# Head norms by logarithm and exponential, in one stage per layer, and plain splits by two engines, in a 32-bit transformer kernel

## What is computed

```
def rms_norm(x, gain):
    xf = x.astype(jnp.float32)
    y = xf * lax.rsqrt(jnp.mean(xf * xf, axis=-1, keepdims=True) + NORM_EPS)
    return (y * gain.astype(jnp.float32)).astype(x.dtype)

q = rms_norm(to_heads(h @ w_q, XM_HEADS), q_norm)
k = rms_norm(to_heads(k, XM_HEADS), k_norm)
...
x = x + from_heads(o) @ w_o
```

## Time and profile before

| | |
|---|---|
| Median of 3 runs | 5059.5 us (5055.14 to 5059.69) |
| Profiled execution, its own time | 5057.54 us |
| Its span | 5055.7 us |
| TensorE products, busy | 4678.1 us (93%) |
| VectorE, busy | 2261.2 us (45%) |
| ScalarE, busy | 1444.6 us (29%) |
| GpSimd, busy | 1938.2 us (38%) |
| Granted TensorE clock, mean | 0.963 |

### The profile page before, as it was taken

The page is one execution under the profiler, slowest core; times in us unless marked ns, Lnnn a source line. Parts: engine busy times, 40 slices in busy tenths (PEclk is TensorE's granted clock), DMA queues, the critical chain, the costliest instruction groups (busy, mean ns, idle before and its releaser), DMA issues. The chain is left out here.

```text
span 5055.7 us, 51526 instructions
## 1 busy us (share of the span) xinstructions
PE 4678.1 (93%) x19788; PEld 3543.7 (70%) x19788; DVE 2261.2 (45%) x4552; ACT 1444.6 (29%) x2163; POOL 1938.2 (38%) x884
## 2 busy tenths in 40 slices
PE   7667889999999999999999988899999997787999
PEld 6224757888888788888788745668878874355787
DVE  8697346983333233333440253454234136654440
ACT  3302322334444211111322234332222232233321
POOL 3054414446666444444444400334444431012443
PEclk9788989999999999999999989999999999998999
DMA  3011313445545656555222200212222221011222
GB/s 113 25 29 46 111 34 102 132 137 178 175 163 179 200 187 191 184 188 181 88 96 96 96 23 14 84 63 94 93 92 96 95 86 40 17 53 54 90 96 84
DMA packets 213172, 519.23 MB, mean 103 GB/s; under 512 B 16960, under 2 KB 82752, under 8 KB 210112
## 3 DMA queue, kind: packets, MB, share of 16 engines
q1 hardware_dynamic: 128448, 448.82, 27.0%
q10 hardware_dynamic: 84480, 67.12, 4.2%
HBM read 446.66 MB, written 69.21 MB: 102 GB/s over the span
## 5 line engine op out<-in xcount | busy, mean ns | idle before, releaser
L187 POOL TENSOR_TENSOR ring_rounded<-ring,highs_rounded 128x1024 fp32r<-128x1024 f32 x687 | 1683.7, 2452 | 2767.2 <-ACT highs_rounded L181 2767.2
L395 PE MATMUL bank<-arena_rounded,ring_rounded 128*128 128x512 f32 (+1 forms) x4488 | 1790.9, 399 | 99.6 <-DVE hT_rounded L413 41.4
L397 PE MATMUL bank<-arena_rounded,highs_rounded 128*128 128x512 f32 (+1 forms) x4488 | 1776.9, 396 | 0.0
L181 ACT ACTIVATE highs_rounded<-ring 128x1024 fp32r<-128x1024 f32 x687 | 727.9, 1061 | 2107.3 <-PE bank L397 1605.5
L396 PE MATMUL bank<-hT_rounded,highs_rounded 128*128 128x512 f32 x3128 | 1228.5, 393 | 0.0
L395 PEld LDWEIGHTS bank<-arena_rounded,ring_rounded 128*128 128x128 f32 x4488 | 854.0, 190 | 293.4 <-issue 86.1
L397 PEld LDWEIGHTS bank<-arena_rounded,highs_rounded 128*128 128x128 f32 x4488 | 852.6, 190 | 205.1
L396 PE MATMUL bank<-arena_rounded,highs_rounded 128*128 128x512 f32 (+1 forms) x2112 | 821.5, 389 | 0.0
L396 PEld LDWEIGHTS bank<-hT_rounded,highs_rounded 128*128 128x128 f32 x3128 | 593.3, 190 | 141.4
L396 PEld LDWEIGHTS bank<-arena_rounded,highs_rounded 128*128 128x128 f32 x2112 | 402.1, 190 | 86.9
L1248 DVE TENSOR_TENSOR arena<-qT,arena 128x512 f32<-128x512 f32 x64 | 150.6, 2354 | 372.2 <-ACT qT L1213 371.6
(11 more groups left out here) (325 smaller groups left out, 4684.9 us busy)
## 6 DMA issues: line engine op xcount, KB each, us to landing
ring<-pages_in SPq DMA_DIRECT2D x687, 512.0 KB, 3.4
act_table<-arena SPq DMA_DIRECT2D x128, 256.0 KB, 4.0
gate_table<-qT SPq DMA_DIRECT2D x16, 2048.0 KB, 7.3
arena<-act_table ACTq DMA_DIRECT2D x128, 256.0 KB, 4.0
arena<-gate_table ACTq DMA_DIRECT2D x32, 1024.0 KB, 8.4
arena<-ssm_in SPq DMA_DIRECT2D x16, 256.0 KB, 2.6
arena<-mem_in SPq DMA_DIRECT2D x3, 1024.0 KB, 4.8
xT<-x_in SPq DMA_DIRECT2D x8, 256.0 KB, 6.4
```

The source lines that it names most:

```text
L181: nc.scalar.activation(f32r(page_high(p)), slot(p), ACT.Copy).then_inc(masked_pages.sem, 1)
L187: nc.gpsimd.tensor_tensor(f32r(slot(p)), slot(p), part_of(page_high(p)), ALU.subtract).then_inc(split_pages.sem, 1)
L395: low_last = nc.tensor.matmul(out, f32r(w_low), f32r(x_high), start=start, stop=False)
L397: return low_last, nc.tensor.matmul(out, f32r(w_high), f32r(x_high), start=False, stop=stop)
```

## The change

It has three parts.

1. In `head_norm` the stage begins with a load of the set that holds both logarithm and exponential. After the last sum, ScalarE takes the logarithm of mean plus epsilon and then the exponential of minus half of it. VectorE makes mean plus epsilon while the exponential runs, and then does the Newton step. The reciprocal is gone.
2. `head_norm` takes units of different lengths. The queries and keys of the memory attention and of the two cross attentions are normed in one stage. There are 8 stages now.
3. In the plain split ScalarE makes the high parts, ahead of its page copies, and VectorE only subtracts.

```diff
-        def inverse_root(link, rms, psum, scale, eps, a, b):
-            link(nc.vector.tensor_scalar(a, psum, scale, eps, ALU.mult, ALU.add))
-            link(nc.vector.reciprocal(rms, rms))
-            link(nc.vector.tensor_tensor(b, rms, rms, ALU.mult))
-            link(nc.vector.scalar_tensor_tensor(out=b, in0=b, scalar=-0.5, in1=a, op0=ALU.mult, op1=ALU.mult))
-            link(nc.vector.scalar_tensor_tensor(out=rms, in0=b, scalar=1.5, in1=rms, op0=ALU.add, op1=ALU.mult))
...
@@ project, ScalarE @@
                         done += min(count, 3)
+                    elif split:
+                        for k in range(nk):
+                            nc.scalar.activation(f32r(high(k)), src(k), ACT.Copy).then_inc(masked_h.sem, 1)
                     for use, part, b, j, need in blocks():
...
@@ project, VectorE @@
                     elif split:
 
-                        for k in range(nk + 1):
-                            if k < nk:
-                                masked(high(k), src(k)).then_inc(masked_h.sem, 1)
-                            if k >= 1:
-                                dve.wait_ge(masked_h.sem, masked_h.at(k))
-                                nc.vector.tensor_tensor(f32r(src(k - 1)), src(k - 1), part_of(high(k - 1)),
-                                                        ALU.subtract).then_inc(h_split.sem, 1)
+                        for k in range(nk):
+                            dve.wait_ge(masked_h.sem, masked_h.at(k + 1))
+                            nc.vector.tensor_tensor(f32r(src(k)), src(k), part_of(high(k)),
+                                                    ALU.subtract).then_inc(h_split.sem, 1)
...
-        def head_norm(units, n, width, rope=None, at=(0, 3584), newton=newton):
+        def head_norm(units, width, rope=None, at=(0, 3584), newton=newton):
...
-            rms = small[0:32, 0:n]
+            rms = small[0:32, :]
+            mean = newton[0:32, 0, :]
             count = len(units)
+            long = [unit[0][0].shape[1] for unit in units]
...
                 def _(act):
+                    nc.scalar.preload_act_table_set("natural_log_exp_and_others")
                     for u, (chunks, window, gain) in enumerate(units):
...
-                            last = nc.scalar.activation(sq[:, u % 2, c, 0:n], ch, ACT.Square)
+                            last = nc.scalar.activation(sq[:, u % 2, c, 0:long[u]], ch, ACT.Square)
...
-                    nc.scalar.activation(rms, bank[0][0:32, 0:n], ACT.Sqrt, bias=gcol("eps")[0:32],
-                                         scale=1.0 / width).then_inc(rooted.sem, 1)
+                    nc.scalar.activation(rms, bank[0][0:32, :], ACT.Ln, bias=gcol("eps")[0:32],
+                                         scale=1.0 / width).then_inc(act_step.sem, 1)
+                    act.wait_ge(act_step.sem, act_step.at(1))
+                    nc.scalar.activation(rms, rms, ACT.Exp, scale=-0.5).then_inc(rooted.sem, 1)
...
+                    dve.wait_ge(act_step.sem, act_step.at(1))
+                    nc.vector.tensor_scalar(mean, bank[0][0:32, :], 1.0 / width, EPS, ALU.mult, ALU.add)
                     dve.wait_ge(rooted.sem, rooted.at(1))
-                    inverse_root(link, rms, bank[0][0:32, 0:n], 1.0 / width, EPS, newton[0:32, 0, 0:n],
-                                 newton[0:32, 1, 0:n])
+                    b = newton[0:32, 1, :]
+                    link(nc.vector.tensor_tensor(b, rms, rms, ALU.mult))
+                    link(nc.vector.scalar_tensor_tensor(out=b, in0=b, scalar=-0.5, in1=mean, op0=ALU.mult,
+                                                        op1=ALU.mult))
+                    link(nc.vector.scalar_tensor_tensor(out=rms, in0=b, scalar=1.5, in1=rms, op0=ALU.add,
+                                                        op1=ALU.mult))
                     dve.sem_inc(inverted.sem, 1)
...
-        head_norm([([Q(2 * h), Q(2 * h + 1)], ALL, "mem_q_g") for h in range(4)], SEQ, 256)
-        head_norm([([kT[:, 2 * h, 0:MEM], kT[:, 2 * h + 1, 0:MEM]], ALL, "mem_k_g")
-                   for h in range(4)], MEM, 256)
+        head_norm([([Q(2 * h), Q(2 * h + 1)], ALL, "mem_q_g") for h in range(4)]
+                  + [([kT[:, 2 * h, 0:MEM], kT[:, 2 * h + 1, 0:MEM]], ALL, "mem_k_g") for h in range(4)], 256)
...
-            head_norm([([Q(h)], ALL, f"xm_q_norm{layer}") for h in range(4)], SEQ, 128)
-            head_norm([([kT[:, h, 0:MEM]], ALL, f"xm_k_norm{layer}") for h in range(4)], MEM, 128)
+            head_norm([([Q(h)], ALL, f"xm_q_norm{layer}") for h in range(4)]
+                      + [([kT[:, h, 0:MEM]], ALL, f"xm_k_norm{layer}") for h in range(4)], 128)
```

More of the change, by code:

```diff
@@ L743, in _ @@
                         for c in range(len(chunks)):
-                            last = nc.tensor.matmul(bank[0][0:32, 0:n],
+                            last = nc.tensor.matmul(bank[0][0:32, 0:long[u]],
                                                     mats[:, WINDOW, window + 30 - 2 * u:window + 62 - 2 * u],
-                                                    sq[:, u % 2, c, 0:n], start=(u == 0 and c == 0),
-                                                    stop=(u == count - 1 and c == len(chunks) - 1))
+                                                    sq[:, u % 2, c, 0:long[u]], start=(u == 0 and c == 0),
+                                                    stop=(u == count - 1 and c == len(chunks) - 1),
+                                                    skip_group_check=True)
                         last.then_inc(summed.sem, 1)
@@ L757, in _ @@
                                 pe.wait_ge(weighed.sem, weighed.at(u - 2))
-                            nc.tensor.matmul(bank[1 + u % 3][:, 0:n], spread[:, u, :], small[:, 0:n], start=True,
+                            nc.tensor.matmul(bank[1 + u % 3][:, 0:long[u]], spread[:, u, :], small[:, 0:long[u]], start=True,
                                              stop=True).then_inc(full.sem, 1)
@@ L764, in _ @@
                                 pe.wait_ge(turned.sem, turned.at(u - 3))
-                            nc.tensor.matmul(bank[4 + (u - 1) % 3][:, 0:n], mat(rope[0]), units[u - 1][0][0],
+                            nc.tensor.matmul(bank[4 + (u - 1) % 3][:], mat(rope[0]), units[u - 1][0][0],
                                              start=True, stop=True).then_inc(rotated.sem, 1)
@@ L772, in _ @@
                     for r in range(32, P, 32):
-                        nc.vector.memset(small[r:r + 32, 0:n], 0.0)
+                        nc.vector.memset(small[r:r + 32, :], 0.0)
+                    dve.wait_ge(act_step.sem, act_step.at(1))
+                    nc.vector.tensor_scalar(mean, bank[0][0:32, :], 1.0 / width, EPS, ALU.mult, ALU.add)
                     dve.wait_ge(rooted.sem, rooted.at(1))
-                    inverse_root(link, rms, bank[0][0:32, 0:n], 1.0 / width, EPS, newton[0:32, 0, 0:n],
-                                 newton[0:32, 1, 0:n])
+                    b = newton[0:32, 1, :]
[4 more added lines that the diff above has]
+                                                        op1=ALU.mult))
                     dve.sem_inc(inverted.sem, 1)
@@ L783, in _ @@
                                 last = nc.vector.scalar_tensor_tensor(
-                                    out=ch, in0=ch, scalar=gcol(gain, c), in1=bank[1 + u % 3][:, 0:n],
+                                    out=ch, in0=ch, scalar=gcol(gain, c), in1=bank[1 + u % 3][:, 0:long[u]],
                                     op0=ALU.mult, op1=ALU.mult)
@@ L790, in _ @@
                             dve.wait_ge(copied.sem, copied.at(u - 2))
-                            nc.vector.tensor_tensor(ch, ch, rest[:, (u - 3) % 2, 0:n], ALU.add)
+                            nc.vector.tensor_tensor(ch, ch, rest[:, (u - 3) % 2, :], ALU.add)
                         if rope is not None and 2 <= u < count + 2:
@@ L794, in _ @@
                             dve.wait_ge(rotated.sem, rotated.at(u - 1))
-                            nc.vector.tensor_tensor(rest[:, (u - 2) % 2, 0:n], bank[4 + (u - 2) % 3][:, 0:n],
+                            nc.vector.tensor_tensor(rest[:, (u - 2) % 2, :], bank[4 + (u - 2) % 3][:],
                                                     rope[2], ALU.mult).then_inc(turned.sem, 1)
@@ L802, in head_norm @@
             rooted.close(1)
+            act_step.close(1)
             inverted.close(1)
@@ L1857, in build @@
         head_norm([([Q(c)], PAIR, "att_q_g") for c in range(4)]
-                  + [([K(c)], PAIR, "att_k_g") for c in range(4)], SEQ, 64, at=(10496, 12544),
+                  + [([K(c)], PAIR, "att_k_g") for c in range(4)], 64, at=(10496, 12544),
                   newton=hT[:, 4:6, :])
@@ L1946, in build @@
         head_norm([([Q(c)], PAIR, "diff_q_norm") for c in range(4)]
-                  + [([K(c)], PAIR, "diff_k_norm") for c in range(4)], SEQ, 64,
+                  + [([K(c)], PAIR, "diff_k_norm") for c in range(4)], 64,
```

(4 more changed lines are left out.)

## The result

The changed kernel takes 5010.2 us (median of four runs, 5005.1 to 5014.9) against 5059.6 for the kernel before in the same comparison. The ratio is 0.9904, with a 95% interval of 0.9886 to 0.9921. That is 49 us faster, where the prediction had 59.5. The profiled execution took 5013.5 us, with a span of 5011.7: 44 us less than the span before.

A forecast was written before the change was run, and what follows sets the result against it. TensorE, busy 93% of the span, bounds the kernel, so only its idle or lower-clock time can be won. 16.8 + 23.7 + 19 = 59.5 us off 5057.5 gives 4998, or 5000 us by the median; range 4980 to 5021.

The forecast's parts named there:

- rival 1: Plain splits: GpSimd holds VectorE's two-input subtraction instead of the cast; 2 us return per stage, 12 lost, 5012 us; 10%.
- Part A: Head norm chain, 8 stages: 3.38 us leave the path, a 1.29 us load is added in front; 16.8 us gained.
- Part B: Three head norm merges: 38.6 us of second stages vanish, 14.9 of keys' work moves into the first; 23.7 us gained.
- part C: Six plain split stages: held cast gone, VectorE's pace per tile falls from 0.93 to 0.63 us; 19 us gained.
- The clock around the head norms: Eight head norm stages: at most 19 us gained by faster restarts against 8 lost before the sum products; set at zero.
- The drain: Head norm table load: the skill's 2.66 us price would cut the gain by 11 us; the trace's 1.29 was taken.
- the four short terms: Plain splits other than memory attention and even layer: one short lower-clock stretch each; gains of 2.4, 2.4, 2.4 and 2.1 us.
- The rivals of the table set and of no effect: Attention: reloads between Exp and Copy, all 352 some 5390 us, 2%; no effect: a dropped load, 1.3 us, inside the forecast.

The follow-up runs named there:

- e9: The changed kernel once more, instruction for instruction, for a second trace; 5007.9 us.
- e4: The changed kernel with ScalarE's first page copy ahead of its high-part copies in the plain split; 5029.4 us.
- e3: The changed kernel with the old square root and reciprocal chain back and no new load, merges and new splits kept; 5019.6 us.
- e1: The changed kernel with each head norm stage's table load moved behind the last Square; 4992.7 us.
- e7: The changed kernel with a second table load (square root's set) ahead of the first in the 8 head norm stages; 5020.0 us.
- e2: The kernel before with the plain split alone changed; 5032.7 us.
- e5: The changed kernel with the three merges undone, eleven head norm stages again, each with its own load in front; 5040.9 us.
- e8: e1 with the plain split as before the change; 5015.5 us.
- e6: e1 with the three merges undone; 5016.9 us.

## Why the prediction was right, and where it was not

It was right in sign and range (4980 to 5021) and 10 us too low. 5010 is also near the 5012 of rival 1, but no subtraction was held, so that is chance. The sum of 59.5 can be laid beside the stages of the two traces of the changed kernel:

| | Predicted | First trace | e9 |
|---|---|---|---|
| Head norm stages (parts A and B) | 40.5 | 32.5 | 38.0 |
| Plain split stages (part C) | 19 | 19.3 | 17.6 |
| All other stages | 0 | -7.7 | -5.9 |
| Span | 59.5 | 44.1 | 49.7 |

*Part A, the chain.* 3.38 us was predicted to leave the path and 3.43 did; 1.29 us was predicted for the load and 1.30 was found. Timed, the part gave 9.3 us instead of 16.8. The step that failed is the one headed "The clock around the head norms", set at zero "from two sides". It weighed less idle time behind the chain (up to 19 us gained) against more idle time in front (8 lost). The second was real, and in two traces of the size given: the sum products of the eight stages take 85.4, 84.5 and 80.7 us in the three traces that have the changed head norms (the first, e9 and e4), against 76.5 in e3. The first came in part, and not in the same stages each time: the spread products, with the rotations, take 139.9, 134.3 and 133.6 us, against 142.8 in the one trace of e3. In the first trace they restart at the lower level, or fall to it within 0.7 us, in every one of the eight stages, although TensorE's idle time there is 3.7 us instead of 7.2. In e9 those of the even layer and of the output norm run at a granted clock of 1.00. So, measured against e3, the two sides came to 6 us lost in the first trace, next to nothing in e9 and 5 us gained in e4. Zero lay among them, but it was no bound, and it hid what e1 shows: with the load behind the squares the loss in front is not there. e1 and the changed kernel differ by 17.6 us timed, of which 8.0 are the load's length and 9.6 are left for the clock.

*The drain.* The Trainium skill (ScalarE: Activation LUTs, "What ACT_TABLE_LOAD costs") gives 2.66 us for a switch of sets with its drain. By that e7 would have cost 21 us; it cost 9.7. ScalarE was idle before the first of its two loads and not before the second. In e1 the load stands right behind a Square, and the next operation starts 1.30 us after it. So no run here shows the drain.

*Part B.* 23.7 us predicted, from the lengths of the old key stages. The three merged stages gave 22.0 in the traces with the old chain (e2 and e3) and 20.7 with the new chain and the load hidden, so these lengths were read about rightly. With the load in front they gave 27.5, since the merges also take three of its eleven copies out. Timed, the same three comparisons gave 13.1, 24.2 and 30.6; the difference from the stages' own share lies in other stages and in which executions were traced. The prediction treated A and B as independent. They are not: it credited A with 8 stages only because B had cut them to 8, and never priced A without B, which e5 and e2 show to be a loss.

*Part C.* 19 us predicted, 19.3 in the six stages of the first trace. They are spread otherwise: the memory attention gave 3.3 instead of 4.7, because its first products ran partly at the lower level (in e2, at full clock, it gave 4.8), and the four short terms of 2.1 to 2.4 each gave 2.5 to 2.9. Timed alone the split gave 27.1 (e2), and 22.9 on top of e1 (e8). ScalarE's copies are 0.52 us apart, not the 0.63 taken, which changes nothing, because VectorE's 0.60 sets the pace. Rival 1, the held subtraction, is a real mechanism (e4) that the order of the program avoids, with a margin of 0.4 us in the stages of eight tiles: GpSimd starts that long after the last subtraction has started. The Trainium skill (SBUF — State Buffer, "SBUF: two separate sides") says that such a pair excludes each other; the 2.42 to 2.44 us of e4 agree.

*The other stages.* The 7.7 us that they lost in the changed kernel's trace, and the 5.9 in e9, were in no term: the prediction looked at the clock only in the stages that it edits. e9 shows that the largest piece, 4.05 us of the stick breaking stage, comes and goes between executions of one program. Another piece goes with the change: the memory attention takes 36.83 us, at a granted clock of 1.00, in the two traces that have the old head norms (before and e2), and 38.30 to 38.61, with a stretch at the lower level, in the other ten. How much of the remainder is the change's own doing, and what sets it off, stays open.

For this reason, and because A and B depend on each other, the parts do not add up: 9.3, 30.6 and 27.1 (or 22.9) make over 60, and 49 were timed. Along one order they must: the split first gives 27.1 (e2), the merges on top 13.1 (e3), the new chain on top 9.3, together 49.5.

*The rivals of the table set and of no effect* did not occur. The changed kernel has the 8 new loads at line 720 and none inside attention; the 7 at the start of attention and the 3 before the square root of the head norms are gone, and all others stand where they stood. (That rival's sum is off: 352 loads of 1.28 us on 5000 give 5450, not 5390.)

## What to carry to other kernels

A table load in front of the first instruction of a stage costs its length; the same load behind the last instruction that another engine still has to work on costs almost nothing (0.2 to 0.6 us of 1.28). Here the move was worth a third again of the whole gain. Before a one-time cost is put at the head of a stage that starts with TensorE idle, look at the granted clock of the first products: the cost may be paid twice, once in its length and once in the clock. When VectorE and GpSimd both work from SBUF, the order in which a third engine releases them decides which one waits.

## What the runs showed that was not expected

The stages of one execution differ from those of another execution of the same program by up to 4 us each, although the totals agree within 0.2%. Where a window was taken over such a stage, the granted clock was what differed. So one trace each is not enough to credit a part with a few us in this kernel. The five head norm stages that were not merged gave 2.8 us in the first trace of the changed kernel and 9.9 in e9 (24.49 instead of 26.32, 37.60 instead of 39.94, 15.75 instead of 18.59, the latent halves nearly unchanged). In e4's trace, whose head norms are the same code, they gave 13.1. With the load behind the squares (e1, e6, e8) the same five gave 17.5 to 20.0 in every trace.
